# Triangular-inverse levels of a two-block kernel: the next matrix and its transpose both made from X plus one

## The reference, cut to what matters

```
def step(state, inp):          # per head, 256 steps, 8 heads of 64
    r_t, w_t, k_t, v_t, kk_t, a_t = inp
    sa = jnp.einsum('bhvk,bhk->bhv', state, -kk_t)
    state = (state * w_t[:, :, None, :] + sa[..., None] * (kk_t * a_t)[:, :, None, :]
             + v_t[..., None] * k_t[:, :, None, :])
    return state, jnp.einsum('bhvk,bhk->bhv', state, r_t)
```

## Time and profile before

| | |
|---|---|
| median of 3 runs | 1488.8 us (1488.18 to 1488.94) |
| the profiled execution's own time | 1483.84 us |
| its span in the trace | 1481.6 us |
| granted TensorE clock, mean | 0.994 of full speed |
| PE, DVE, ACT busy | 1405.8, 802.7, 572.9 us |
| largest group of PE by line | L538, every matmul that `mm` issues |

### The profile page before, as it was taken

One profiled execution on the slowest core, in us unless ns is written; L12 is line 12 of the kernel. 1 busy time (PEld: TensorE's weight loads), 2 busy tenths in 40 slices (PEclk: granted clock), 3 DMA queues, 4 the chain that ended last, 5 costly groups with the idle time before them and its releaser, 6 DMA issues.

```text
span 1481.6 us, 24690 instructions
## 1 busy us (share of the span) xinstructions
PE 1405.8 (95%) x10704; PEld 1017.2 (69%) x10704; DVE 802.7 (54%) x1186; ACT 572.9 (39%) x880; POOL 52.4 (4%) x43
## 2 busy tenths in 40 slices
PE   6999999999899999999999999988999999998898
PEld 6887454453786444443788877787788978777776
DVE  4766111211756111212777876577757886775764
ACT  4542111111441111111456485643545556664342
POOL 0010000001020000000000000010000000001000
PEclk9999999999899999999999999999999999999999
DMA  9548999999369999998353343500554433432032
GB/s 376 169 148 344 421 424 421 423 422 406 115 238 373 380 421 422 423 422 334 124 181 131 115 138 114 187 15 3 171 214 152 140 120 132 160 114 87 4 115 85
DMA packets 47490, 340.26 MB, mean 230 GB/s; under 512 B 5296, under 2 KB 5296, under 8 KB 7568
## 3 DMA queue, kind: packets, MB, share of 16 engines
q1 hardware_dynamic: 45504, 328.03, 57.2%
q0 software_dynamic: 1872, 10.57, 1.9%
HBM read 337.53 MB, written 1.05 MB: 229 GB/s over the span
## 4 chain that ended last, share of the span: by engine, by line
PE 81%; DVE 9%; ACT 7%; issue 2%; DMA 1%; SPq 0%; DVEq 0%
PE bank L538 46%; PE bank L901 15%; PE bank L942 8%; PE bank L845 4%; PE bank L544 2%; ACT arena L1628 2%; DVE d_lo L1856 2%; ACT d_hi L1444 2%; PE bank L874 1%; PE bank L541 1%; PE bank L879 1%; ACT arena L1405 1%; DMA ring<-wsecond 1%; DVE arena L2282 1%; PE bank L884 1%
## 5 line engine op out<-in xcount | busy, mean ns | idle before, releaser
L1856 DVE TENSOR_TENSOR d_lo<-ring,d_hi 128x2048 fp32r<-128x2048 f32 (+2 forms) x111 | 249.3, 2254 | 98.3 <-ACT d_hi L1444 98.1
L1444 ACT ACTIVATE d_hi<-ring 128x2048 fp32r<-128x2048 f32 (+2 forms) x115 | 216.0, 1887 | 142.7 <-PE bank L538 115.6
L538 PE MATMUL bank<-arena 64*64 64x64 f32 (+7 forms) x3168 | 168.5, 238 | 18.4 <-issue 6.0
L1405 ACT ACTIVATE arena<-bank 128x512 f32<-128x512 f32 (+4 forms) x222 | 108.2, 496 | 188.8 <-PE bank L538 111.9
L538 PE MATMUL bank<-xT_hi,d_hi 128*128 128x256 f32 x592 | 167.2, 282 | 2.2 <-ACT arena L1724 1.7
L538 PE MATMUL bank<-d_hi,xT_hi 128*128 128x512 f32 (+1 forms) x400 | 158.5, 396 | 9.1 <-ACT arena L1666 4.0
L538 PEld LDWEIGHTS bank<-arena 64*64 64x64 f32 (+4 forms) x3168 | 137.4, 140 | 43.0 <-issue 17.7
L538 PE MATMUL bank<-xT_hi,d_lo 128*128 128x256 f32 x592 | 166.2, 281 | 0.0
L538 PE MATMUL bank<-xT_lo,d_hi 128*128 128x256 f32 x592 | 165.7, 280 | 0.0
L538 PE MATMUL bank<-d_hi,xT_lo 128*128 128x512 f32 (+1 forms) x400 | 157.4, 394 | 0.0
L538 PE MATMUL bank<-d_lo,xT_hi 128*128 128x512 f32 (+1 forms) x400 | 156.4, 391 | 0.0
(11 more groups left out here) (357 smaller groups left out, 2056.8 us busy)
## 6 DMA issues: line engine op xcount, KB each, us to landing
ring<-wmoe SPq DMA_DIRECT2D x84, 1024.0 KB, 16.8
ring<-wsecond SPq DMA_DIRECT2D x80, 1024.0 KB, 4.8
arena<-wmoe SPq DMA_DIRECT2D x72, 1024.0 KB, 17.0
ring<-wfirst SPq DMA_DIRECT2D x30, 1024.0 KB, 4.9
wide<-wmoe SPq DMA_DIRECT2D x24, 1024.0 KB, 19.7
xT_raw<-wmoe SPq DMA_DIRECT2D x12, 1024.0 KB, 19.9
rows<-lnrows POOLq DMA_DIRECT2D x4, 1024.0 KB, 7.8
ring<-wsecond SPq DMA_DIRECT2D x4, 848.0 KB, 10.5
```

Of the source, the lines that this page charges most:

```text
L538: mark(nc.tensor.matmul(o, lhsT, rhs, start=start, stop=stop, skip_group_check=loose), full)
L1405: nc.scalar.activation(o, bank_ap, func).then_inc(bank_free[b], act.sends(bank_free[b]))
L1444: nc.scalar.activation(high_of(u)[:, 0:width], raw[u % NRAW][:, 0:width], ACT.Copy).then_inc(sem("piece_high"), 1)
L1856: v.tensor_tensor(d_lo[u % NRAW][:, 0:width], raw[u % NRAW][:, 0:width], high_of(u)[:, 0:width], SUB).then_inc(sem("piece_low"), 1)
```

## The change

Per level and parity, DVE now adds one to X on its way out of PSUM (`with_unit`: Xm = bank par + unit), and PE makes T (X + 1) and its transpose from it, TTm by Xm into the first 256 columns of bank 5+par and Xm by TTm into the next 256. ACT copies all 512 columns at once to `both_turns`, in which Tm and TTm now lie side by side. `level_turn` is gone, with its bank 7. X goes to bank par. The mask of the next level is one operation over both parities (512 columns), behind both additions of one; `level_start` masks both parities at once too. After the last level DVE makes X plus one and ACT copies TTm, where before ACT copied Xm and DVE added to TTm. On DVE, both low parts of mg4 move ahead of `merge(sgm)`, and `add_merged` moves from before tile 0 to between levels 3 and 4 of tile 0. AkT and AbT lie elsewhere and are dense.

```diff
--- before.py
+++ after.py
@@ -341,10 +341,13 @@
         assert cl.at <= FREE_A
...
         cl = Carve(FREE_B)
-        KnMv, AkT, AbT = cl(NH, P), chunked(cl(2, 4, P)), chunked(cl(2, 4, P))
+        KnMv = cl(NH, P)
         assert cl.at <= KEYS
         cl = Carve(KEYS_END)
-        Tm, TTm = chunked(cl(2, 4, P)), chunked(cl(2, 4, P))
+        both_turns = cl(2, 4, P).rearrange("p a b c -> p a (b c)")
+        in_halves = both_turns.rearrange("p a (h b c) -> p a h b c", h=2, b=4)
+        Tm, TTm = in_halves[:, :, 0, :, :], in_halves[:, :, 1, :, :]
+        AkT, AbT = cl(2, 4, CH), cl(2, 4, CH)
         WU = cl(2, 4, P)
...
         Vn, Bn, Kp = (cl(MIX) for _ in range(3))
@@ -361,7 +364,7 @@
         states = [oT_flat[:, g * 256:(g + 1) * 256] for g in range(3)]
...
         GT, Hs = flat2(Nl[:, 0, :, :]), flat2(Nl[:, 1, :, :])
-        QT = v3(Tm.rearrange("p a b c -> p (a b c)"), 4)
+        QT = v3(both_turns[:, 0, :], 4)
         yv = klT[:, :, 0:P]
...
 
@@ -1202,7 +1205,6 @@
                 merge_values(f"pb.{l}", 4 * l + 2)
...
                 done()
-                turned = [None, None]
 
...
 
@@ -1229,37 +1231,29 @@
                                 cs = of_chunk(c)
...
 
-                def level_x(par, lev):
-
-                    pe_eng.wait_ge(sem("level_ready"), pe.next("level_ready"))
-                    pe_eng.wait_ge(bank_free[5 + par], pe.reuse(5 + par))
+                def level_x(par):
+
+                    if par == 0:
+                        pe_eng.wait_ge(sem("level_ready"), pe.next("level_ready"))
+                    pe_eng.wait_ge(bank_free[par], pe.reuse(par))
                     for j in range(4):
...
                             cs = of_chunk(c)
-                            mm(banks[5 + par][cs, j * CH:(j + 1) * CH], Nl[cs, par, j, :], Tm[cs, par, j, :], full=5 + par if j == 3 and c else None)
-                    pe.note(f"x{par}.{lev}.{l}.{tt}", 5 + par)
+                            mm(banks[par][cs, j * CH:(j + 1) * CH], Nl[cs, par, j, :], Tm[cs, par, j, :], full=par if j == 3 and c else None)
 
...
 
-                    pe_eng.wait_ge(bank_free[5 + par], pe.used(5 + par))
-                    if turned[par]:
-                        pe_eng.wait_ge(bank_free[7], turned[par])
-                    pe_eng.wait_ge(bank_free[par], pe.reuse(par))
-                    left, right = (Xm, TTm) if last else (TTm, Xm)
+                    pe_eng.wait_ge(bank_free[par], pe.used(par))
+                    pe_eng.wait_ge(bank_free[5 + par], pe.reuse(5 + par))
+                    if not last:
+                        for j in range(4):
+                            for c in range(2):
+                                cs = of_chunk(c)
+                                mm(banks[5 + par][cs, j * CH:(j + 1) * CH], TTm[cs, par, j, :], Xm[cs, par, j, :])
                     for j in range(4):
...
                             cs = of_chunk(c)
-                            mm(banks[par][cs, j * CH:(j + 1) * CH], left[cs, par, j, :], right[cs, par, j, :], full=par if j == 3 and c else None)
-
-                def level_turn(par):
-
-                    pe_eng.wait_ge(bank_free[par], pe.used(par))
-                    pe_eng.wait_ge(bank_free[7], pe.reuse(7))
-                    for j in range(4):
-                        for c in range(2):
-                            cs = of_chunk(c)
-                            tr_chunk(banks[7][cs, j * CH:(j + 1) * CH], Tm[cs, par, j, :], c, full=7 if j == 3 and c else None)
-                    turned[par] = pe.used(7)
+                            mm(banks[5 + par][cs, (4 + j) * CH:(5 + j) * CH], Xm[cs, par, j, :], TTm[cs, par, j, :], full=5 + par if j == 3 and c else None)
 
...
 
@@ -1294,17 +1288,16 @@
                             for c in range(2):
...
                                 tr_chunk(banks[b][cs, j * CH:(j + 1) * CH], TTm[cs, par, j, :], c, full=b if j == 3 and c else None)
-                    turned[0] = turned[1] = None
                     pe_eng.wait_ge(bank_free[7], pe.used(7))
-                    level_x(0, 1)
-                    level_x(1, 1)
+                    level_x(0)
+                    pe_eng.wait_ge(bank_free[6], pe.used(6))
+                    level_x(1)
                     for lev in range(1, LEVELS - 1):
...
                         level_t(1, False)
-                        level_turn(0)
-                        level_x(0, lev + 1)
-                        level_turn(1)
-                        level_x(1, lev + 1)
+                        for par in range(2):
+                            pe_eng.wait_ge(bank_free[5 + par], pe.used(5 + par))
+                            level_x(par)
                         if lev == 1:
...
                             chunk_values()
@@ -1778,12 +1771,6 @@
                 key_mix(l, 1)
...
 
-                def level_x(par):
-                    copy_out(Xm[:, par, :, :], 5 + par, v3(banks[5 + par][:, 0:4 * CH], 4))
-
-                def level_turn(par):
-                    copy_out(TTm[:, par, :, :], 7, v3(banks[7][:, 0:4 * CH], 4))
-
                 for tt in range(TT):
...
                     copy_out(NTm[:, 1, :, :], 6, v3(banks[6][:, 0:4 * CH], 4))
@@ -1797,17 +1784,15 @@
                     copy_out(Kp, 7, banks[7][:, :])
...
                     copy_out(Tm[:, 1, :, :], 6, v3(banks[6][:, 0:4 * CH], 4))
-                    level_x(0)
-                    level_x(1)
                     for lev in range(1, LEVELS - 1):
-                        level_turn(0)
-                        level_x(0)
-                        level_turn(1)
-                        level_x(1)
+                        for par in range(2):
+                            copy_out(both_turns[:, par, :], 5 + par, banks[5 + par][:, :])
                         if tt == 0 and lev > 1:
...
                             roots(NH)
+                    for par in range(2):
+                        copy_out(TTm[:, par, :, :], 5 + par, v3(banks[5 + par][:, 4 * CH:8 * CH], 4))
                     copy_out(WU[:, 1, :, :], 6, v3(banks[6][:, :], 4))
...
                         high_to(f"mg4.{l}", 2)
@@ -2407,17 +2392,21 @@
                 scaled(lw[tt], pinv).then_inc(dve_step, dve.sends(dve_step))
...
 
+            def level_mask(lev):
+                mask = bc(cst[:, C_LEV + lev * CH:C_LEV + (lev + 1) * CH].unsqueeze(1), P, 8, CH)
+                return v.tensor_tensor(Nl.rearrange("p a b c -> p (a b) c"), NTm.rearrange("p a b c -> p (a b) c"), mask, MUL)
+
             def level_start(l, tt):
...
                     dve_eng.wait_ge(bank_free[b], free)
-                    v.tensor_tensor(Nl[:, par, :, :], NTm[:, par, :, :], mat4(C_LEV), MUL).then_inc(dve_step, dve.sends(dve_step))
-                    dve_eng.wait_ge(dve.last, dve.value)
+                level_mask(0).then_inc(dve_step, dve.sends(dve_step))
+                dve_eng.wait_ge(dve.last, dve.value)
+                for par in range(2):
                     v.tensor_tensor(TTm[:, par, :, :], Nl[:, par, :, :], mat4(C_UNIT), ADD).then_inc(sem("level_ready"), dve.sends(sem("level_ready")))
                 dve_eng.wait_ge(dve.last, dve.value)
-                for par in range(2):
-                    v.tensor_tensor(Nl[:, par, :, :], NTm[:, par, :, :], mat4(C_LEV + CH), MUL).then_inc(sem("level_ready"), dve.sends(sem("level_ready")))
+                level_mask(1).then_inc(sem("level_ready"), dve.sends(sem("level_ready")))
 
...
                 for par in range(2):
@@ -2425,17 +2414,14 @@
                     dve_eng.wait_ge(bank_full[b], dve.next(("full", b)))
...
 
-            def level_add(l, tt, lev):
-                for par in range(2):
-                    b, full, _ = BANK_USE[f"x{par}.{lev}.{l}.{tt}"]
-                    dve_eng.wait_ge(bank_full[b], full)
-                    v.tensor_tensor(Nl[:, par, :, :], NTm[:, par, :, :], mat4(C_LEV + (lev + 1) * CH), MUL).then_inc(sem("level_ready"), dve.sends(sem("level_ready")))
-                add_to(Tm)
-
-            def add_to(dst):
+            def level_add(lev):
+                with_unit()
+                level_mask(lev + 1).then_inc(sem("level_ready"), dve.sends(sem("level_ready")))
+
+            def with_unit():
                 for par in range(2):
                     dve_eng.wait_ge(bank_full[par], dve.next(("full", par)))
-                    v.tensor_tensor(dst[:, par, :, :], dst[:, par, :, :], v3(banks[par][:, 0:4 * CH], 4), ADD).then_inc(bank_free[par], dve.sends(bank_free[par]))
+                    v.tensor_tensor(Xm[:, par, :, :], v3(banks[par][:, 0:4 * CH], 4), mat4(C_UNIT), ADD).then_inc(bank_free[par], dve.sends(bank_free[par]))
 
...
                 if n:
@@ -2622,31 +2608,31 @@
                 key_sum(4)
...
                 mixed_keys(1)
-                low_to(f"mg3.{l}", 2)
+                low_to(f"mg3.{l}", 4)
                 merge(sgm, False)
-                add_merged(sgm)
 
...
                     masked(MTm, 0, C_STRICT)
-                    level_add(l, tt, 1)
```

(13 more changed lines are left out.)

## The result

The changed kernel takes 1477.24 us (median of 4, 1475.5 to 1478.05) against 1488.49 us (1484.8 to 1488.94) for the kernel before beside it: ratio 0.9927, 95% interval 0.9908 to 0.9946, so 8 to 14 us less. The forecast was 1483.5 with a range of 1479.8 to 1487.3: the direction was right, the gain was twice as large, and the range misses it. The profiled execution's own time is 1478.05, its span 1475.9, against 1483.84 and 1481.6. That lies beside the 1478.5 forecast for this execution, but by luck: as the table shows, the stretches that were changed gave more than forecast, and code that wasn't touched took more time in this execution.

What follows compares the result with a forecast made beforehand. TensorE, busy 95%, was taken as the bound, with level waits on ACT and DVE; 2 layers x (1.95 + 0.71) = 5.3 us off the 1488.8 median gave 1483.5, range 1479.8 to 1487.3.

Steps and rivals of the forecast that it cites:

- item 3: Tile 1, walked through DVE's queue: WU starts 18.20 us after the first x instead of 20.15, saving 1.95 per layer.
- the base: Offset from profiled execution to median, 5.0 us (median 1488.8), carried over to put the forecast at 1483.5 instead of 1478.5.
- item 2: Round trips in a level through ACT's 512-column copy: 3.33 us against 3.40, so 0.07 saved per level.
- Items 1, 5 and 6: PE product groups per level unchanged; add_merged leaving tile 0's head gains 0; mg4 lows ahead of merge cost 0.
- Item 4: Tile 0: WU at 18.01 us from the first x instead of 18.72; 0.71 saved, add_merged's 0.75 delay counted.
- Items 7 and 8: Single mask for both parities costs 0, ending 0.7 us early; GpSimd slows masks, not PSUM additions, 0.07 taken.
- rival C: DVE less late than walked, a queued pair taking 0.74 not 0.84; both tiles end 1 us earlier: 1479.5, chance 0.12.
- A: Groups of t step 0.52 us, not 0.45, so levels gain up to 0.35; about 3.5 of 5.3 lost: 1487, chance 0.17.
- B: Only the moved low part counts, 1.55 us a layer: 1485.7, at the edge of no change, chance 0.11.
- D: Masks come onto PE's path in all 8 levels of a layer, 5.7 us slower: 1494.5, chance 0.08.

Runs made afterwards that it cites:

- d1: Changed kernel with its new levels, but low parts and add_merged where they stood before: 1482.38 us, ratio 0.9969.
- e3: Changed kernel with add_merged right behind the MTm masks at the head of tile 0 instead of between levels 3 and 4: 1477.66 us (single).
- e4: Changed kernel with the 512-column mask of every level made twice, 0.7 us more on DVE per level: 1489.59 us (single).
- b1: Kernel before with only both low parts of mg4 moved ahead of merge(sgm): 1485.18 us, ratio 0.9988.
- c1: Kernel before with the low parts and add_merged moved, levels as before: 1484.92 us, ratio 0.9984.
- f3: Changed kernel with two unread 128 x 512 products in TensorE's wait at the head of tile 0: 1476.17 us, ratio 0.9927.

## Why the prediction was wrong in size

Two terms were mis-sized, and both made the forecast time too long. The walk charged DVE too much for operations that wait in its queue (item 3), and the forecast took the 5.0 us between the profiled execution and the median as a constant (the base). A third, smaller one is the round trip of item 2, which tells in tile 0.

**Items 1, 5 and 6, the start of tile 0: right.** PE's instructions are 10704 as before; the head is 7.08 with and without the addition; merge still waits for ACT, and the second low part ends 1.90 us before it, which is the cover forecast to the digit. DVE of the changed kernel, last layer:

```profile
1337.91 2.29 DVE L1841 TENSOR_TENSOR d_lo<-ring,d_hi 128x2048 fp32r<-128x2048 f32 x1 [3.27 <-ACT d_hi L1437]
1342.10 2.48 DVE L2318 TENSOR_TENSOR arena<-bank,arena 128x512 f32<-128x512 f32 x4 [1.90 <-ACT small L1647]
```

**Item 2, the level: nearly.** From 1396.46 to 1399.70 is 3.24 us, forecast 3.33. The copy takes what was forecast; PE starts 0.05 us after it (1399.05 + 0.60, ACT below), for which I had 0.12. From the end of t's last group to x of parity 1 are 0.86 us (1398.84 to 1399.70), where 1.00 was charged; a group takes 0.47 instead of 0.45, which gives some of it back. Copies of ACT in tile 1 of the last layer:

```profile
1398.12 0.60 ACT L1398 ACTIVATE arena<-bank 128x512 f32<-128x512 f32 x1 [0.19 <-PE bank L541]
1399.05 0.60 ACT L1398 ACTIVATE arena<-bank 128x512 f32<-128x512 f32 x1 [0.34 <-PE bank L541]
```

**Item 3, tile 1: the step that failed.** WU starts 17.27 us after the first x, at 1401.43 (forecast 18.20, before 20.15). The walk had DVE late twice, with its addition of level 3 at 9.7 us and gn_scale's end at 16.5, and so a wait of 0.9 us on PE behind level 2 and a short one before the last t. DVE of the changed kernel, tile 1 of the last layer, first x at 1384.16:

```profile
1389.04 0.74 DVE L2424 TENSOR_TENSOR arena<-bank,cst 128x256 f32<-128x256 f32 x2
1389.70 0.68 DVE L2397 TENSOR_TENSOR arena<-arena,cst 128x512 f32<-128x512 f32 x1
1390.30 0.74 DVE L2415 TENSOR_TENSOR arena<-bank,cst 128x256 f32<-128x256 f32 x2
...
1393.20 0.42 DVE L2424 TENSOR_TENSOR arena<-bank,cst 128x256 f32<-128x256 f32 x1
...
1399.69 0.42 DVE L2424 TENSOR_TENSOR arena<-bank,cst 128x256 f32<-128x256 f32 x1
```

From the additions of a level to the next operation are 1.26 us (1389.04 to 1390.30). I charged 0.42 + 0.42 + 0.69 = 1.53. Operations that wait in DVE's queue overlap: the pair steps by 0.66, the mask by 0.60, though one addition lasts 0.42 and the mask 0.68 by itself. The earlier trace rows showed this before (a pair in 0.74), and I used it for rival C only. Over two levels it is 0.5 us, and the masks, gn_mean and gn_square between them are 0.16 shorter than charged. So the addition of level 3 came at 9.04 instead of 9.7, the one behind gn_scale at 15.53 instead of 16.5, and of the wait of 0.9 us the 0.16 inside the row of 1393.05 is left. t of level 3 starts at 9.52, 0.61 earlier than walked; by x of parity 1 for level 5 the lead is 0.69, and at WU 0.93, as the wait behind gn_scale isn't there either. 20.15 - 17.27 is 2.88, the 2.93 of the table.

**Item 4, tile 0: short for another reason.** WU starts at 17.61 (1367.95 from 1350.34) against 18.01. The addition's delay was right in its mechanism and its size (0.75 forecast, 0.77 by d1 and e3). What it was subtracted from was not: the levels alone are worth 1.94, where 1.46 had been walked. DVE's queue isn't what makes that difference, as d1 shows: its levels 3 to 5 in tile 0 list no wait for DVE, and WU still starts 0.4 before its walk (16.86 from the first x; 18.01 less the delay is 17.26). It is the pace of the level, 3.24 to 3.25 us in the rows of d1 and of the changed kernel against 3.33, four times, and 0.07 that was taken for GpSimd and isn't there.

**Items 7 and 8: right.** PE waits for no mask, though the one that GpSimd held ends at 1357.53, 0.57 us before x of level 3 (1358.10), so the cover there is a little under the 0.7 forecast; e4 used it up. DVE of the changed kernel in tile 0 of the last layer, then GpSimd's two operations beside it:

```profile
1355.31 0.74 DVE L2424 TENSOR_TENSOR arena<-bank,cst 128x256 f32<-128x256 f32 x2
1355.97 1.56 DVE L2397 TENSOR_TENSOR arena<-arena,cst 128x512 f32<-128x512 f32 x1
1357.45 0.74 DVE L2415 TENSOR_TENSOR arena<-bank,cst 128x256 f32<-128x256 f32 x2
```

```profile
1355.94 1.04 POOL L2752 TENSOR_TENSOR arena<-arena 128x512 f32<-128x512 f32 x1
1357.06 1.42 POOL L2754 TENSOR_TENSOR arena<-arena,rows 128x512 f32<-128x512 f32 x1
```

The mask was held for 0.88 us, the additions from PSUM not at all, and PE's next wait is the usual 0.23. The Trainium skill's page "SBUF — State Buffer", section "Who interferes with whom", says that a VectorE operation with two SBUF inputs contends with a GpSimd one that reads SBUF, and that one with at most one SBUF input doesn't, outside the perf modes that take two ports. The trace agrees with both halves (1.56 us against 0.68 for the mask, 0.74 for the pair of additions), as it did before the change.

**The base.** This is the other term that failed. The forecast took 5.0 us between profile and median as given, from three runs. Over 60 runs of the kernel before its median is 1486.7, 2.8 above its first profile; the four profiled executions have 1483.84, 1486.62, 1486.0 and 1487.9 us, mean 1486.1. Those of the changed kernel have 1478.05, 1476.7 and 1477.98, mean 1477.6. The difference of these means is 8.5 us, that of the segments from the merge to mg4 (before 144.8, 146.7, 146.8 and 147.4 us for both layers, changed 137.3, 138.5 and 139.4) 8.0. The medians of the three sets differ by 11.25, 9.7 and 10.0. Of the forecast's 6.3 us error, 2.9 are the walk (8.2 instead of 5.3), 2.2 the offset (5.0 instead of 2.8), and 1.2 are left, less than the scatter of the changed kernel's 16 runs (1474.28 to 1478.05 us). Whether the medians hold 1 to 2 us more than the segments isn't settled; with three and four profiled executions the means are themselves uncertain by as much.

**Why half the change seemed worth little.** By the ratios the parts are worth -1.8 (low alone), -2.4 (moves) and -4.6 us (levels), against -11.7 for the whole in the same set, while in the segments moves and levels make 8.7 against 8.2. Each run has a mean granted clock, and it differs: 23 of the 36 runs of the three half-changed kernels are below 0.992, 4 of the 29 of the kernel before in the same set (11 of 60 in all sets), 1 of 16 of the changed one. A line fitted through the 142 runs of the kernels that ran more than once, with one constant per kernel and one slope, has 0.79 us (0.66 to 0.93) per 0.001 of clock, and at equal clock the low part is worth 4.0 us, the moves 3.6, the levels 6.1 and the whole 10.3, each give or take 1.0. Moves and levels make 9.7, so nothing that can be told is lost between them. That the mean clock is lower in the half-changed kernels is measured; why isn't. The wait of 1.98 us in d1 has a fall behind it in one layer and none in the other (1.99), and in b1 and c1, which have no wait before WU, the mean clock is as low.

**The rivals.** C described what happened in tile 1, where the end came 1.0 us earlier than walked, for the reason that it named. In tile 0 it was 0.5, and for the other reason of item 4. In the segments C's 9.3 us are more than the 8.2 measured; its 1479.5 is still above 1477.24 because it stands on the same offset. A is out: t groups step as x groups do (96 records in 3.02 us, 0.031 each). B is what b1 measured, and only part of the whole. D didn't come, but e4 shows it 0.7 us of DVE work a level away.

## What to carry to other kernels

When a walk through an engine's queue is the argument, charge a queued operation by the step from its start to the next one's start, read from a row with a count of two or more, and not by its duration alone; each makes 0.08 us of difference here, ten make 0.8, and that decided whether PE waits. A part of a change is to be weighed by its segment in the trace as well as by its median, because the mean granted clock can differ between two versions (here 0.9904 to 0.9943) and cover a gain of 2 us. Where TensorE must wait over a microsecond for another engine, one product that nobody reads is a cheap trial: it took 3.0 us off the kernel before, while the trial in the changed kernel (f3, two products) showed nothing clear.
